# Second kind of block: the feed-forward norm's root moved behind its products, and a first group of six products

## What is computed

```
def rms_norm_2(x, g):
    y = x * rsqrt(mean(x * x, axis=-1) + EPS)
    return y * g

h = h + rms_norm_2(mixed @ w_out, g_mix_post)                        # norm m2
gate, up = split(rms_norm_2(h, g_ffn_pre) @ w_ffn_in, 2)             # norm m3
h = h + rms_norm_2((silu(gate) * up) @ w_ffn_out, g_ffn_post)        # norm m4
e = p_i @ w_ple_proj
h = h + rms_norm_2(sigmoid(h @ w_ple_gate) * e, g_ple_post)          # norm m5
```

## Time and profile before

| what | value |
|---|---|
| median of 3 runs | 4047.55 us (4045.89 to 4049.76) |
| the profiled execution's own time | 4045.97 us |
| its span, first to last instruction | 4044.2 us |
| TensorE matmuls | busy 3757.4 us, 93% of the span |
| VectorE | busy 1830.2 us, 45% |
| ScalarE | busy 829.1 us, 21% |
| GpSimd | busy 2247.9 us, 56% |
| mean granted TensorE clock | 0.966 |

### The profile page before, as it was taken

How to read it: one execution, slowest core, us unless ns; L and a number is a source line. 1 busy time by engine, 2 the same in 40 slices (tenths; PEclk the granted TensorE clock), 3 DMA queues, 4 the chain that set the end, 5 groups by cost and what they waited for, 6 DMA issues and landing times.

```text
span 4044.2 us, 52799 instructions
## 1 busy us (share of the span) xinstructions
PE 3757.4 (93%) x21204; PEld 3029.4 (75%) x21204; DVE 1830.2 (45%) x2504; ACT 829.1 (21%) x1286; POOL 2247.9 (56%) x2218
## 2 busy tenths in 40 slices
PE   5799899999799899999899999999998999999997
PEld 4577578887577578888787667888777776778886
DVE  5845564244954563123733545212365535542124
ACT  2221110002212110002421432000243225220002
POOL 4421667786421667774555345777644463557773
PEclk9899999999899999998999998999989999989998
DMA  4222344342122344332223222333222231323332
GB/s 183 78 68 84 120 150 143 117 154 79 59 64 79 123 154 123 97 97 66 73 79 110 63 82 80 95 98 97 94 63 69 75 115 50 105 71 98 97 97 68
DMA packets 192194, 386.06 MB, mean 95 GB/s; under 512 B 21456, under 2 KB 21584, under 8 KB 190288
## 3 DMA queue, kind: packets, MB, share of 16 engines
q1 hardware_dynamic: 169776, 338.24, 27.5%
q10 hardware_dynamic: 22176, 44.45, 3.2%
HBM read 361.64 MB, written 20.97 MB: 95 GB/s over the span
## 4 chain that ended last, share of the span: by engine, by line
PE 81%; DVE 13%; ACT 4%; issue 1%; DMA 1%; ACTq 0%; SPq 0%; DVEq 0%
PE psum L385 17%; PE psum L386 17%; PE psum L387 17%; PE psum L430 3%; PE psum L452 3%; PE psum L432 3%; PE psum L431 2%; PE psum L405 2%; PE psum L406 1%; PE psum L407 1%; PE psum L881 1%; PE psum L856 1%; DVE units L1733 1%; PE psum L538 1%; PE psum L528 1%
## 5 line engine op out<-in xcount | busy, mean ns | idle before, releaser
L2118 POOL TENSOR_SCALAR w_hi<-raw 128x512 fp32r<-128x512 f32 x1082 | 744.1, 688 | 1580.6 <-DMA raw<-weight_chunks 1578.6
L2120 POOL TENSOR_TENSOR w_lo<-raw,w_hi 128x512 fp32r<-128x512 f32 x1082 | 1468.1, 1357 | 90.2
L385 PE MATMUL psum<-in_hi,w_hi 128*128 128x512 f32 x1968 | 785.6, 399 | 30.7 <-ACT zbuf L1044 26.4
L386 PE MATMUL psum<-in_lo,w_hi 128*128 128x512 f32 x1968 | 769.5, 391 | 0.0
L387 PE MATMUL psum<-in_hi,w_lo 128*128 128x512 f32 x1968 | 768.9, 391 | 0.0
L385 PEld LDWEIGHTS psum<-in_hi,w_hi 128*128 128x128 f32 x1968 | 371.9, 189 | 124.0 <-ACT zbuf L1044 28.3
L386 PEld LDWEIGHTS psum<-in_lo,w_hi 128*128 128x128 f32 x1968 | 372.0, 189 | 84.2 <-issue 8.5
L387 PEld LDWEIGHTS psum<-in_hi,w_lo 128*128 128x128 f32 x1968 | 371.5, 189 | 77.9
L430 PE MATMUL psum<-in_hi,w_hi 128*128 128x512 f32 x576 | 262.8, 456 | 42.5 <-ACT gate_st L1018 33.0
L432 PE MATMUL psum<-in_hi,w_lo 128*128 128x512 f32 x576 | 229.3, 398 | 0.0
L431 PE MATMUL psum<-in_lo,w_hi 128*128 128x512 f32 x576 | 229.3, 398 | 0.0
(11 more groups left out here) (409 smaller groups left out, 6662.2 us busy)
## 6 DMA issues: line engine op xcount, KB each, us to landing
raw<-weight_chunks SPq DMA_DIRECT2D x1082, 256.0 KB, 2.6
ada_col<-ada_slabs SPq DMA_DIRECT2D x80, 512.0 KB, 4.2
spill<-gate_st ACTq DMA_DIRECT2D x56, 256.0 KB, 2.8
ada_at<-ada_slabs SPq DMA_DIRECT2D x8, 1024.0 KB, 15.7
gin<-spill ACTq DMA_DIRECT2D x32, 256.0 KB, 3.2
mgs<-spill ACTq DMA_DIRECT2D x32, 256.0 KB, 2.9
sml<-small ACTq DMA_DIRECT2D x4, 1024.0 KB, 6.2
spill<-nt ACTq DMA_DIRECT2D x16, 256.0 KB, 2.5
```

The source lines that it names most:

```text
L385: pe.matmul(bank[:], wh, hi[:, i, :], start=(i == 0), stop=False)
L386: pe.matmul(bank[:], wh, lo[:, i, :], start=False, stop=False)
L2118: ts(w_hi[:, slot, :], raw[:, slot, :], 1.0, 1.0, ALU.mult, ALU.mult).then_inc(sem("chunk_hi"), 1)
L2120: ins = tt(w_lo[:, slot, :], raw[:, slot, :], w_hi[:, slot, :].bitcast(F32), ALU.subtract)
```

## The change

It has three parts, all in the second kind of block, so each happens twice, once for each layer.

1. Norm m3. The inputs of the feed-forward's first products are now x times g, without the root. ScalarE makes the high part straight from the new tile of `x`, and `post_norm` makes the low part as soon as a tile is there. The root is taken while the products run, kept in a new tile `rs_t`, and VectorE multiplies each of the 44 output tiles by it. The silu is then taken in place from SBUF, and VectorE multiplies gate by up in an instruction of its own.
2. `late_group`: the first group has six products (gate and up 0 to 2), in three "lin" banks, the "bg" bank and two "aux" banks. Before its last tile come the token sums of m3, and in the middle of the last tile the transposes. The eight sums of `parts=True` are replaced by three, with `add_square` on VectorE.
3. Norm m4. Its token sums come after two of the eight products "pe" and its transposes after four. ScalarE makes the first four high parts between the evacuations of the last four products. The splits of the inputs of "pe" move on VectorE from ahead of the feed-forward to the end of its first half.

```
+            def late_group(l, members, pools):
+                key = ("m3", l)
+                banks = [begin(name, pool, "late") for (name, _, _, _), pool in zip(members, pools)]
+                for k in range(DT):
+                    ready = ("split_ready", ("m3", l, k))
+                    if k == DT - 1:
+                        norm_tokens(key)
+                    pe.wait_ge(sem(ready[0]), count(*ready))
+                    seen.add(ready)
+                    for n, ((name, matrix, _, m), bank) in enumerate(zip(members, banks)):
+                        if k == DT - 1 and n == len(members) // 2:
+                            norm_spread(key)
+                        wh, wl = next_block((matrix, l, k, m))
+                        pe.matmul(bank[:], wh, in_hi[:, k, :], start=(k == 0), stop=False)
+                        pe.matmul(bank[:], wh, in_lo[:, k, :], start=False, stop=False)
+                        ins = pe.matmul(bank[:], wl, in_hi[:, k, :], start=False, stop=(k == DT - 1))
...
                 norm_sum(("m2", l))
-                norm_sum(("m3", l), parts=True)
                 h_in3 = lambda i: ("split_ready", ("m3", l, i))
-                group([(("eg", l, 0), "w_ffn_in", l, 0), (("eu", l, 0), "w_ffn_in", l, HT),
-                       (("eg", l, 1), "w_ffn_in", l, 1)], h_in3)
+                late_group(l, [((n, l, m), "w_ffn_in", l, m0 + m) for m in range(3) for n, m0 in (("eg", 0), ("eu", HT))],
+                           ("lin", "lin", "lin", "bg", "aux", "aux"))
...
                 for m in range(DT):
+                    if m == PE_BEFORE_SUM:
+                        norm_tokens(("m4", l))
+                    if m == PE_BEFORE_SPREAD:
+                        norm_spread(("m4", l))
                     projection(("pe", l, m), "w_ple_proj", l, m, lambda i: ("split_ready", ("pp", l, i)),
                                kt=2, hi=pp_hi, lo=pp_lo)
-                norm_sum(("m4", l))
...
-                squares(("m3", l))
-                norm_root(("m3", l))
-                high_parts(("m3", l))
+                key = ("m3", l)
+                for i in range(DT):
+                    act.wait_ge(sem("x_tile"), count("x_tile", (key, i)))
+                    af(in_hi[:, i, :], x[:, i, :], ACT.Copy, scale=col2(l, "g_ffn_pre", i)).then_inc(sem("hi_ready"), 1)
+                    act.wait_ge(sem("hi_ready"), passed("hi_ready", (key, i)))
+                    if i >= 3:
+                        act.wait_ge(sem("sq_added"), count("sq_added", (key, i - 2)))
+                    af((sqd[i % 2] if i else ssq)[:], x[:, i, :], ACT.Square).then_inc(sem("sq_ready"), 1)
+                    act.wait_ge(sem("sq_ready"), passed("sq_ready", (key, i)))
+                norm_root(key)
                 for mm in range(HT):
-                    job = ("eg", l, mm)
-                    if mm >= 2:
-                        act.wait_ge(sem("split_ready"), count("split_ready", ("h2", l, (mm - 2) // HALF, (mm - 2) % HALF)))
-                    act.wait_ge(*done(job))
-                    af(hs2[mm % 2][:, 0, :], bank_of(job)[:], ACT.Silu).then_inc(bank_read(job), 1)
-                    act.wait_ge(bank_read(job), turn(job))
+                    gate = hs2[mm % 2][:, 0, :]
+                    act.wait_ge(*moved(("eg", l, mm)))
+                    af(gate, gate, ACT.Silu).then_inc(sem("silu_ready"), 1)
+                    act.wait_ge(sem("silu_ready"), passed("silu_ready", (l, mm)))
...
                 for m in range(DT):
+                    if m == PE_BEFORE_SUM:
+                        norm_root(("m4", l))
                     job = ("pe", l, m)
                     act.wait_ge(*done(job))
                     af(ee[:, m, :], bank_of(job)[:], ACT.Copy).then_inc(bank_read(job), 1)
                     act.wait_ge(bank_read(job), turn(job))
+                    if m >= PE_BEFORE_SPREAD:
+                        high_part(high)
+                        high += 1
...
+                    if i and then == ("m3", l):
+                        j = i - 1
+                        dve.wait_ge(sem("hi_ready"), count("hi_ready", (then, j)))
+                        ins = stt(in_lo[:, j, :], x[:, j, :], col2(l, "g_ffn_pre", j), in_hi[:, j, :].bitcast(F32),
+                                  ALU.mult, ALU.subtract)
+                        ins.then_inc(sem("split_ready"), 1)
+                        dve.wait_ge(sem("split_ready"), passed("split_ready", then + (j,)))
+                        add_square(then, j)
...
-                normed_inputs(("m3", l), cols_of(l, "g_ffn_pre"))
-                for i in range(2):
-                    split(sml[:, 1 + i, :], pp_hi[:, i, :], pp_lo[:, i, :], ("pp", l, i))
+                rs = spread_root(("m3", l))
+                job = ("rs", ("m3", l))
+                dve.tensor_copy(rs_t[:], rs[:]).then_inc(bank_read(job), 1)
...
-                        tt(h[:, 1, :], h[:, 0, :], bank_of(job)[:], ALU.mult).then_inc(bank_read(job), 1)
-                        dve.wait_ge(bank_read(job), turn(job))
+                        for i, n in enumerate(("eg", "eu")):
+                            job = (n, l, mm)
+                            dve.wait_ge(*done(job))
+                            tt(h[:, i, :], bank_of(job)[:], rs_t[:], ALU.mult).then_inc(bank_read(job), 1)
+                            dve.wait_ge(bank_read(job), turn(job))
+                        dve.wait_ge(sem("silu_ready"), count("silu_ready", (l, mm)))
+                        tt(h[:, 1, :], h[:, 0, :], h[:, 1, :], ALU.mult).then_inc(sem("vector_step"), 1)
+                        dve.wait_ge(sem("vector_step"), passed("vector_step"))
                         split(h[:, 1, :], h2_hi[:, m, :], h2_lo[:, m, :], ("h2", l, f, m))
+                    if f == 0:
+                        for i in range(2):
+                            split(sml[:, 1 + i, :], pp_hi[:, i, :], pp_lo[:, i, :], ("pp", l, i))
```

40 lines of the change are left out of this document (28 added, 12 removed).

## The result

| | before | changed |
|---|---|---|
| median of 4 runs | 4048.66 us (4045.89 to 4050.32) | 4026.16 us (4023.49 to 4027.36) |
| ratio, 95% interval | | 0.9944 (0.9927 to 0.9961) |
| the profiled execution | 4045.97 us | 4025.8 us, span 4023.7 |

The account below looks back on a forecast made before the run. TensorE was taken as the bound (81% of the chain), waiting at two places in each of two layers. 2 x (14.4 + 5.0) = 38.8 us off gave 4009 us, 8-in-10 range 4001 to 4021.

Parts of the forecast that it names:

- m3, forecast 14.4: Norm m3: first product 16.6 us sooner, 3.15 paid for sums and transposes, 0.95 back at the group's end; 14.4 a layer.
- the restart at the lower level costs 2.0 us as it does now and cancels: Start of m3's first group: ten slow matmuls at 0.20 us extra each, before and after the change alike.
- The feed-forward's steps: VectorE's added work per step stays hidden under TensorE's 10.88 us a step; no gain or loss.
- the next never is: VectorE in the feed-forward: only the first SBUF instruction of a run is slow; the next took 691 to 694 ns.
- Rival (b): Every SBUF instruction of VectorE waits for GpSimd; 7 us lost a layer in m3, m4 at 2.5, 4028 us; chance 6%.
- the cover that was named: Feed-forward: TensorE's products hide VectorE's added instructions and the silu wait, otherwise about 2.5 us x 22 a layer.
- (a): VectorE late behind the group of six; TensorE waits 3 us a layer for a bank, m4 gives 2.5; 4020 us; chance 15%.
- (c): The group of six starts early but is fed at VectorE's pace, about 7 us later a layer; 4023 us; chance 3%.
- (d): Slower than before: VectorE's feed-forward step outgrows TensorE's 10.88 us; at 12 us a step, 4058 us; chance 2%.
- Norm m4, forecast 5.0: Norm m4: `post_norm` 6.8 us sooner, group pg 3.9 sooner; gain 2.5 to 6.7 us a layer, 5.0 taken.
- 22 taken: VectorE's string in norm m4, 20.5 us before, was taken as 22 with GpSimd at work all the way.
- the bad branch of my own bounds: Norm m4's last group: TensorE alone done at 2911.2 us if its clock falls in the 1.4 us pause, otherwise 2909.2.

Follow-up runs that it names:

- m3 alone: The changed kernel with norm m4 as in the kernel before; 4031.84 us against 4050.35, ratio 0.995.
- m4 alone: The kernel before with only the norm m4 part of the change, the moved splits left out; 4046.85 us against 4050.35, ratio 0.999.
- sums short: The changed kernel with only 8 of the 24 token-sum matmuls (first of three tiles) in m3 and m4; 4016.72 us in one execution.

## Why the prediction was wrong, step by step

**m3, forecast 14.4, measured 13.4 a layer.** The mechanism held. The first product is 4.02 us behind the first update (4.02), the sums with TensorE cost 2.57 us (2.59), no wait stands behind the group, and none for a bank in m3. In m3 alone the stage is the same, so it owes nothing to m4. The term that was mis-sized is "the restart at the lower level costs 2.0 us as it does now and cancels". In m3 of the changed kernel 8 to 13 matmuls are slow in all, in two of its four executions five of them behind the sums, and by the distances between starts (the first left out) this costs 1.8 to 2.8 us where before it was 1.4 to 1.9. More than some ten matmuls at the lower level was one of my signs of being wrong. A fall behind the sums slows the transposes too (1.05 us in the timeline of the first profile, 0.60 in the row above). Where they were only eight, the stage was 368.3 us, a gain of 14.2.

**The feed-forward's steps, forecast nothing: right, by other numbers.** The lines of VectorE in the first layer:

```profile
L2122 DVE TENSOR_TENSOR hs<-hs 128x512 f32<-128x512 f32 x22 | 33.2, 1511 | 2.3 <-ACT hs L1443 1.4
L2119 DVE TENSOR_TENSOR hs<-psum,rs_t 128x512 f32<-128x512 f32 x44 | 30.4, 692 | 111.0 <-PE psum L394 110.7
L1512 DVE TENSOR_TENSOR h_lo<-hs,h_hi 128x512 fp32r<-128x512 f32 x22 | 24.9, 1134 | 0.8
L1510 DVE CAST h_hi<-hs 128x512 fp32r<-128x512 f32 x22 | 12.3, 557 | 0.8
```

A step is 2 x 0.69 + 1.51 + 0.56 + 1.13 = 4.6 us, and that after a slow first "the next never is" is wrong here: the product is slow, and so is the low part, which was 691 to 694 in all 22 places before; the cast between them is now the fast one. Rival (b) had half of its mechanism and none of its price. Gate 3 was read at 2557.08, 18.1 us behind the sums (forecast 19 to 20.5, needed at 20.9), and the 110.7 us of waiting for TensorE are the cover that was named. Rivals (a), (c) and (d) did not come.

**Norm m4, forecast 5.0, measured 0.9 a layer: this is the step that failed.** Even my lower bound was 2.5. The sentence "So `post_norm` starts at 2877.35 + 5.44 + 2.59 + 0.73 = 2886.1, 6.8 us sooner", took 12 matmuls between sums and transposes at the upper level. In m4 alone that holds (8.88). In the changed kernel the clock fell there in 8 places of 8, and it was 10.46, once 12.05. VectorE and TensorE of the first layer, timelines:

```profile
2881.97 0.75 DVE L2025 SCALAR_TENSOR_TENSOR nt<-yy,col,psum 128x512 f32<-128x512 f32 x1 [4.37 <-PE psum L518]
...
2888.48 1.64 DVE L2050 TENSOR_TENSOR in_lo<-x,in_hi 128x512 fp32r<-128x512 f32 x1
...
2904.51 1.49 DVE L2050 TENSOR_TENSOR in_lo<-x,in_hi 128x512 fp32r<-128x512 f32 x2
```

```profile
2890.01 0.47 PE L436 MATMUL psum<-in_hi,w_hi 128*128 128x512 f32 x1 [2.70 <-ACT ee L1458]
2898.93 0.50 PE L436 MATMUL psum<-in_hi,w_hi 128*128 128x512 f32 x1 [0.47 <-DVE in_lo L2050]
2902.13 0.50 PE L436 MATMUL psum<-in_hi,w_hi 128*128 128x512 f32 x1 [0.86 <-DVE in_lo L2050]
2905.26 0.50 PE L436 MATMUL psum<-in_hi,w_hi 128*128 128x512 f32 x1 [0.76 <-DVE in_lo L2050]
```

The string runs 2881.97 to 2906.00, 24.0 us, and 23.4 over the eight places, against 22 taken (bounds 20.5 to 25) and 20.0 before. GpSimd's low parts are most of the difference: without them it is 19.8. The group starts at 18.5 us (forecast 15.5) behind a bank that ScalarE reads only after a high part, and then waits tile by tile for VectorE, which is what the three last rows show. In sum, of the 4.1 us missing a layer, 2.4 are what m4 alone keeps and the changed kernel doesn't (72.6 - 70.2), the fall of the clock and the longer string behind it. The other 1.7 (5.0 - 3.3) are missing in m4 alone too. Its string ended 0.6 later than forecast, its group started 1.1 later (16.6), and it restarted at the lower level, the bad branch of my own bounds. Its m5 came 38.8 us behind the end of the string on average, where before the change it was 37.9; I had counted on the same distance.

Why the string lengthens shows in GpSimd's timeline beside VectorE's row at 2888.48 above (its 1.64 us instead of 0.69):

```profile
2887.91 1.66 POOL L2189 TENSOR_TENSOR w_lo<-raw,w_hi 128x512 fp32r<-128x512 f32 x1
...
2890.76 1.30 POOL L2189 TENSOR_TENSOR w_lo<-raw,w_hi 128x512 fp32r<-128x512 f32 x1
2896.01 0.62 POOL L2187 TENSOR_SCALAR w_hi<-raw 128x512 fp32r<-128x512 f32 x1 [3.95 <-DMA raw<-weight_chunks]
```

VectorE's low part starts while GpSimd's runs and ends 0.55 us behind its end (2890.12 against 2889.57), about its own length. While GpSimd waits for a chunk, 2892.06 to 2896.01, VectorE's low parts take the bare 0.69 us (at 2892.64 and 2894.88). The Trainium skill (SBUF — State Buffer, section Who interferes with whom) states such an exclusive lock for VectorE's instructions with two SBUF inputs, against a GpSimd instruction that reads SBUF. The trace agrees here, with 1175 and 974 ns that became 830 and 777 without GpSimd's low parts, and 747 that stayed 748 where an input is in PSUM. It doesn't settle which instruction of a run waits: the low part behind the cast has two SBUF inputs and took 691 to 694 ns in 22 of 22 before.

**The sum.** By stages 28.5 instead of 38.8: 2 x 1.0 in m3 and 2 x 4.1 in m4. The medians on record were 22.5 apart, 26.7 and 26.8 in the two longer comparisons. The changed kernel had 4026.2, 4026.0 and 4026.6 us in the three; the kernel before had 4048.7 on record and 4050.4 to 4053.4 in the later ones. So 28.5 from 4048.7 would be 4020, just inside the range, and the 6 us from there to 4026 lie outside both stages. The profiles say where, but not why. In the four of the changed kernel the first residual update comes 5.2 us later on average than in the two of before (2499.9 against 2494.6), and the stretch from m5 of the first layer to m2 of the second takes 1.2 us longer (624.1 against 622.9); 28.5 - 5.2 - 1.2 = 22.1, and the spans are 22.2 apart. Nothing was edited in these parts, and one kernel's first updates differ by up to 12 us between its executions. But variation need not be all: over all profiles the update stands at 2500.5 in the 14 with the new m3 and at 2495.9 in the 5 without, and the stretch reads 622.5 to 626.2 in the 14 and 622.4 to 623.0 in the 5. That the changed program is a few us slower outside the stages is open. My range had no room for it: its spread came from m4 and from VectorE behind the group of six alone.

**What stays open.** What about its place makes a run of sums bring the clock down. TensorE works without a wait from m3's group to the sums of m4, so the place repeats; the changed kernel and m4 alone differ in how long that stretch is, and a product, 1.36 us, is enough to change the outcome either way. Other places, and a run without any one-column matmul in it, were not tried. That sums short shows no fall can be its length or its place. Also open are the us outside the stages, and why m3 alone gained less by its medians than by its stages.

## What to carry to other kernels

Work put inside a stream of matmuls costs more than its own duration if the granted clock falls behind it, and whether it falls can turn on the place by one product: try two or three places before you judge such a move, and read the granted clock of the stretch behind it, not only the sum matmuls. When a norm is started sooner, its gain ends at the next engine's string; read the distance from the end of that string to the next stage. Where it stays the same (38.3 to 38.5 us in seven places of eight here), a sooner start of anything else brings next to nothing; where it grows (43.7 and 45.0 behind one product with five high parts), something else sets the end. And where executions differ by more than the effect, compare distances between two instructions that enclose the change.

## What the hardware showed that I had not expected

- The same TensorE instructions at the same distances to 0.01 us are followed by the lower clock level in 14 places of 14 in the changed kernel and the variants that keep its m4 sums, and in none of 4 in m4 alone. With the sums 1.36 us later it was there in 4 of 4, two of them in m4 alone, and 1.36 us sooner in none of 4. It cost 1.6 us behind two products, once 3.2, and behind three about 3.2 in the changed kernel (13.4 against 8.88 + 1.36) and 1.6 in m4 alone.
- In VectorE's run of three SBUF instructions in the feed-forward, the first product took 1511 ns on average, the cast behind it 557 and the low part 1134; with the cast first, the cast took up to 1543 and the low part 691 to 694.
- The clock's falls in a restart trade places: in m3 of the changed kernel 13 slow matmuls at the start and none behind the sums, or five to seven and then five, with the same end at 42.9 to 43.2 us; eight and none gave 41.9.
